# Moving weight slabs and their inputs to other byte offsets in on-chip memory

## The reference, cut to what matters

```
q, k, v = split(x @ w_qkv)            # 1024 x 3072, dilated: 1024 x 9216
gate, val = split(x @ w_in)           # 1024 x 5632
y = (gelu(conv(gate)) * val) @ w_out  # 2816 x 1024
x = layer_norm(alpha * x + y)
```

## Time and profile before

| | |
|---|---|
| median of 3 runs | 2066.23 us |
| the profiled execution | 2065.53 us, of which 2063.8 us from first to last instruction |
| TensorE matmul busy | 1916.5 us, 93% |
| GpSimd busy | 1255.1 us, 61% |
| VectorE, ScalarE busy | 1090.8 us, 999.2 us |
| HBM read | 339.65 MB, 165 GB/s over the span |

### The profile page before, as it was taken

How to read it: one execution, slowest core, us unless ns; L and a number is a source line. 1 busy time by engine, 2 the same in 40 slices (tenths; PEclk the granted TensorE clock), 3 DMA queues, 4 the chain that set the end, 5 groups by cost and what they waited for, 6 DMA issues and landing times.

```text
span 2063.8 us, 34083 instructions
## 1 busy us (share of the span) xinstructions
PE 1916.5 (93%) x13629; PEld 1696.5 (82%) x13629; DVE 1090.8 (53%) x1524; ACT 999.2 (48%) x1726; POOL 1255.1 (61%) x583
## 2 busy tenths in 40 slices
PE   7989999998999989989999899898879999998997
PEld 7879788887999866868887788876669987968996
DVE  5473346633610173146667655688665623856981
ACT  4654345543444473435553444378735545625542
POOL 8767566786888405546788334200468886426995
PEclk9999999998999999999999899999989999999999
DMA  6435367864555405358763212221235553324552
GB/s 261 142 142 184 112 259 305 319 258 153 198 190 184 143 1 194 136 216 304 311 250 143 82 64 100 82 82 62 83 132 183 183 184 143 123 82 153 189 194 106
DMA packets 49217, 342.30 MB, mean 166 GB/s; under 512 B 5264, under 2 KB 7312, under 8 KB 8144
## 3 DMA queue, kind: packets, MB, share of 16 engines
q1 hardware_dynamic: 47440, 331.02, 43.6%
q0 software_dynamic: 1664, 9.70, 1.2%
HBM read 339.65 MB, written 1.05 MB: 165 GB/s over the span
## 4 chain that ended last, share of the span: by engine, by line
PE 70%; DVE 14%; ACT 6%; POOL 6%; issue 2%; DMA 2%; DVEq 0%; SPq 0%; ACTq 0%; POOLq 0%
PE bank L1724 13%; PE bank L1726 12%; PE bank L1728 12%; PE bank L1779 10%; POOL w_lo L2232 4%; PE bank L1954 2%; PE bank L1829 2%; PE bank L1326 2%; PE bank L1328 2%; PE bank L1329 2%; PE bank L1756 2%; PE bank L1759 2%; PE bank L1758 2%; DMA ring<-slabs_dram 2%; ACT wh_area L1160 2%
## 5 line engine op out<-in xcount | busy, mean ns | idle before, releaser
L2232 POOL TENSOR_TENSOR w_lo<-ring,w_hi 128x1024 fp32r<-128x1024 f32 x360 | 876.7, 2462 | 287.7 <-ACT w_hi L2821 287.2
L1724 PE MATMUL bank<-x_hi,w_hi 128*128 128x256 f32 x2176 | 616.5, 283 | 18.1 <-POOL w_lo L2232 14.3
L1728 PE MATMUL bank<-x_lo,w_hi 128*128 128x256 f32 x2176 | 610.0, 280 | 0.0
L2821 ACT ACTIVATE w_hi<-ring 128x1024 fp32r<-128x1024 f32 x448 | 448.8, 1052 | 326.1 <-DMA ring<-slabs_dram 319.4
L1724 PEld LDWEIGHTS bank<-x_hi,w_hi 128*128 128x128 f32 x2176 | 417.5, 192 | 38.2 <-issue 36.7
L1728 PEld LDWEIGHTS bank<-x_lo,w_hi 128*128 128x128 f32 x2176 | 413.9, 190 | 0.0
L1726 PE MATMUL bank<-x_hi,w_lo 128*128 128x256 f32 x1472 | 413.4, 281 | 0.0
L1726 PEld LDWEIGHTS bank<-x_hi,w_lo 128*128 128x128 f32 x1472 | 280.9, 191 | 0.0
L2232 POOL TENSOR_TENSOR w_hi<-ring,w_hi 128x1024 fp32r<-128x1024 f32 x88 | 209.0, 2396 | 99.9 <-ACT w_hi L2821 99.9
L2745 ACT ACTIVATE arena<-bank 128x512 f32<-128x512 f32 (+1 forms) x144 | 80.0, 559 | 274.5 <-PE bank L1728 191.0
L1726 PE MATMUL bank<-x_hi,w_hi 128*128 128x256 f32 x704 | 197.1, 280 | 0.0
(11 more groups left out here) (360 smaller groups left out, 3689.0 us busy)
## 6 DMA issues: line engine op xcount, KB each, us to landing
ring<-slabs_dram SPq DMA_DIRECT2D x308, 1024.0 KB, 4.8
lnrow<-ln_dram POOLq DMA_DIRECT2D x6, 1024.0 KB, 5.0
arena<-slabs_dram SPq DMA_DIRECT2D x4, 1024.0 KB, 7.9
xt<-xT_dram SPq DMA_DIRECT2D x1, 1024.0 KB, 5.7
xt<-memT_dram SPq DMA_DIRECT2D x1, 1024.0 KB, 11.9
x<-x_dram SPq DMA_DIRECT2D x1, 1024.0 KB, 13.6
arena<-ctx_dram POOLq DMA_DIRECT2D x1, 1024.0 KB, 7.7
lnrow<-ln_dram POOLq DMA_DIRECT2D x2, 512.0 KB, 4.7
```

The costliest lines, as they stand in the source:

```text
L1724: ins = pe.matmul(dst, wh[:, k, c], src[0][:, k, :], start=(k == 0), stop=False)
L1728: ins = pe.matmul(dst, wh[:, k, c], src[1][:, k, :], start=False, stop=(k == KC - 1))
L2232: pool.tensor_tensor(dst[:, c], ring[:, s, c], w_hi[:, s, c].bitcast(F32), ALU.subtract).then_inc(S["lo_ready"], 1)
L2821: a.activation(w_hi[:, g % RING, c], ring[:, g % RING, c], ACT.Copy) \
```

## The change

Three things are reordered in the allocation. `small` shrinks from 576 to 480 floats, its columns are packed closer, and it goes to the front with 64 unused bytes behind it (`apart`); `pick` gets an area of its own where `small` was; `mod` goes behind the ring. The assertions state the outcome: `xh_area` begins 64 bytes past a multiple of 1024, and `xt2`, and with it `wh_area` and `ring`, on a multiple. By the same sums `tri`, `arena` and `x` are at 64, `dist0`, `dist` and `lnrow` at 576, `xlat`, `xt2`, `wh_area` and `ring` at 0. No instruction is added, removed or moved in any queue.

```diff
+        small = sb("small", [P, 480])
+        sb("apart", [P, 16])
         xh_at = aligned()
+        assert xh_at % 1024 == 64
         xh_area = sb("xh_area", [P, 2048])
...
         row = sb("row", [P, NROW])
-        small = sb("small", [P, 576])
-        mod = sb("mod", [P, 2, 6, 8, 2])
+        pick_area = sb("pick_area", [P, 32])
         sc_in = sb("sc_in", [P, KC, 32])
         xlat = sb("xlat", [P, KC, T])
         xt2_at = aligned()
+        assert xt2_at % 1024 == 0
...
         ring = sb("ring", [P, RING, SLAB])
+        mod = sb("mod", [P, 2, 6, 8, 2])
...
-        pick = small[:, 264:296]
-        modA = small[:, 168:184]
-        lamp = small[:, 312:440]
-        dtn = small[:, 312:568].rearrange("p (t h) -> p t h", t=4)
+        pick = pick_area[:, :]
+        modA = small[:, 152:168]
+        lamp = small[:, 216:344]
+        dtn = small[:, 216:472].rearrange("p (t h) -> p t h", t=4)
```

More of the change, by code:

```diff
@@ L263, in build @@
         half16 = small[:, 136:152]
-        pick = small[:, 264:296]
-        modA = small[:, 168:184]
-        lamp = small[:, 312:440]
-        dtn = small[:, 312:568].rearrange("p (t h) -> p t h", t=4)
[L268 to L276, removed]
+        pick = pick_area[:, :]
+        modA = small[:, 152:168]
+        lamp = small[:, 216:344]
+        dtn = small[:, 216:472].rearrange("p (t h) -> p t h", t=4)
+        epsb = small[:, 472:473]
+        sub_col = small[:, 198:199]
+        qscale = small[:, 168:176]
+        tok_i = small[:, 176:184].bitcast(I32)
+        tok_f = small[:, 184:190]
+        sq = small[:, 190:194].rearrange("p (s t) -> p s t", s=2)
+        var2 = small[:, 194:196]
+        rstd2 = small[:, 196:198]
+        dcol = small[:, 200:216]
         qT = cut(0, 8, T)
@@ L383, in build @@
         pair_sum = part("pair_sum", place(28480, 64), 64)
-        sq4 = small[:, 206:210]
+        sq4 = small[:, 190:194]
         uraw = cut(0, 8, 512)
```

## The result

The change made the kernel slower: 2079.17 us median (2074.1 to 2084.1, five runs) against 2065.68 us for the kernel before (2062.2 to 2067.2, five runs), a ratio of 1.0071 with a 95% interval of 1.0048 to 1.0094. The profile is of an execution of 2074.1 us with a span of 2072.4, the lowest of the five; the profiled execution before took 2065.5.

A forecast was written before the change was run, and what follows sets the result against it. TensorE bounds the kernel through matmul count times step. From 2065.5 us it took 15.5 us for 256-column products leaving the 117.8 ns step and nothing for the rest, giving 2050.0, range 2022 to 2082.

The forecast's parts named there:

- rival B: Every stage: the new offsets suit TensorE worse and all take the 117.8 ns step; 2087 us; chance 0.20.
- What bounds the kernel: Dense stages: TensorE never idles, so time is the number of matmuls times the step from one to the next.
- Term (1): 256-column products: 3926 of 8448 leave the 117.8 ns step for 113.3, 17.3 us, of which 15.5 us shows.
- The step behind it: `swo_tile`, 512 columns: equal offsets give 225 ns a matmul, offsets 192 apart 240; the change brings every 192 to 64.
- Term (2): 512-column products, 2016 at about 229 to 231 ns: taken as nothing; 6.5 us less if all reached 226.6.
- Term (3): Dense stages below 113.3 ns: taken as nothing; a full drop to 106.7 is 56 us, 512 columns 27 more.
- rival C: Dense stages: the new offsets also remove part of the loss in the 113.3 ns step; 2012 us; chance 0.13.
- Rival A: Dense stages: something other than offsets picks the pace, the mix stays about as now; 2066 us; chance 0.25.
- Term (5): `small`, `pick` and `mod` in new places: costed at nothing, bounds below 1 us either way.
- Term (4): Beside TensorE: GpSimd keeps its cover in h0; if DMA refused the faster slabs in f0, 4.6 us would be lost.

The follow-up runs named there:

- the sweep: Separate kernel with TensorE alone on constant data, inputs' offset varied against the weights': 113.3 to 120.0 ns at 256 columns, 226.7 to 233.3 at 512.
- the arena at distance 0: The changed kernel with the arena moved to the weights' offset modulo 256, main inputs still 64 bytes away: 2070.29 us, ratio 1.0042 to the kernel before.
- pauses: Separate kernel with TensorE alone, 256-column groups behind pauses of eight lengths at seven pairs of input and weight places: 113.3, 117.8 or 120.0 ns.
- old offsets: The changed kernel with `small` and `pick_area` behind `row`, inputs at 128 and weights at 960 as before the change: 2065.3 us, ratio 1.0001.
- another 64: The changed kernel with `small` back behind `row`, inputs at 128 and weights at 64: 2081.3 us, ratio 1.0078 to the kernel before.
- distance 0: The changed kernel's packing with `small` behind `row`, inputs and weights both at 128: 2092.24 us, ratio 1.0152 to the kernel before.
- Another 192: The changed kernel with `small` back behind `row`, inputs at 192 and weights at 0: 2062.3 us, ratio 0.9988 to the kernel before.

## Why the prediction was wrong

It said 2050 with a range of 2022 to 2082; the kernel takes 2079. The range holds it, the sign is wrong, and it came out as rival B, which had 0.20.

- **What bounds the kernel** was read rightly: the time was lost in TensorE's step alone, and the experiments reproduce the loss with no other engine at work.
- **Term (1) failed: "the slow pace at 256 columns goes".** It spread. The steady steps of 256 columns cost 17.4 us over the fast pace before and 30.5 us after; by means over three, 53% of them were fast before and 15% after. Of the three places where the prediction looked for the fall, q and k of the second dilated group fell to 113.3, and h0 and f0 did not. The cause is the distance of 64: by the sweep its usual pace with the inputs streaming is 117.8, while 192, the old one, is the best place of all with 113.3. The whole kernel with only the distance changed has the loss (1.0078), and with all but the distance changed has not (1.0001).
- **The step behind it** is the reading of the earlier trace rows: equal offsets 225 ns, 192 apart 240, so closer is better. That is two matmuls a value, from starts rounded to 10 ns, so each may be 5 ns off; over all of L1548 the steps are 228.4 ns with `w_swo` and 233.1 with `w_lo`. And it is one shape at one distance, with the weights streaming, where most products of 256 columns stream the inputs. Distance 0 is indeed the best for 512 columns (226.7; 227.3 in the kernel), but the worst for 256 columns (120.0; 119.9), where most of the time is. And no row was read for a distance of 64, so the value at 64 was a guess between two points of a curve that isn't monotonic. The 240 didn't recur as a steady step: at distance 192 it is 228.8 in the sweep.
- **Term (2), the 512-column products, was taken as 0** and measured +5.7 us: 5.9 us over twice the fast pace before, 11.6 after. The bound "if all went to 231.5, 4 us" was short, since the steady step at 64 is 233.3. With the arena at distance 0 the hidden activations' share of it came back.
- **Term (3) and rival C** (something below the fast pace): nothing did, in 16 + 4 + 6 pairs of equal offsets and 64 unequal combinations. The least is 113.3 at 256 columns; 226.7 at 512.
- **Rival A was half right.** At one distance the phase in which a stretch starts picks between two paces: same addresses, 117.9 and 113.3 (the two blocks shown under pauses). In the whole kernel "old offsets" shows the same, with h0 fast where it was slow at the same places. But the odds belong to the distance: at 192, 30 of 32 blocks with pauses fast; at 64, 15 of 16 slow. The argument "equal addresses, so addresses alone do not pick the pace" was sound, and said nothing on the odds.
- **Rival B's price, 21.5 us, was nine tenths of 19.9 + 4.** The steady steps came to +18.8 and the median to +13.5. The allowance for what borders and waits give back, a tenth, was too small here: in the profiled execution it was 10.0 of 18.8. It isn't a constant: the same subtraction gives 18.2 and -1.3 us for "another 64", 31.4 and -3.8 at distance 0, 14.8 and -9.9 for the arena at 0. What makes it -10 in two of them and -1 in another was not settled. It goes with the mean granted clock of the profiled execution: 0.972 in the two with -10, 0.969 before, 0.970 at distance 0 and 0.967 in "another 64", which over the span is some 12 us less, and up to 9 us more, at the lower level. That is one trace each, so chance of the execution and effect of the addresses aren't told apart.
- **Term (5), the moves at nothing**, held: ratio 1.0001 with both packings compared at equal offsets, and 1.0078 against 1.0071 at distance 64 with `small` behind `row` or at the front. Term (4) was not put to the test, since TensorE got slower; the windows of f0 show 309 GB/s for 314.
- **Smaller readings.** The "32 small matmuls" of an f0 slab are 16 rows in the trace; nothing was worked out from the 32. The 118.3 ns read for `half` is the 117.8 of the slow pace, from starts rounded to 10 ns.

The rule quoted in the prediction, from the Trainium skill, "SBUF — State Buffer", section "Who interferes with whom" (two independent read ports, TensorE waits on no one), would have given 2066. Taken to mean that the operands' places cost TensorE nothing, the measurement decides against it: with no other engine at work, 113.3 to 120.0 ns for the same instructions by where the two operands lie. Which of the two reads is late, no run shows.

## What to carry to other kernels

Where a trace shows the same matmuls at two steps, or a step above its columns over the clock, measure the step over the operands' places (here 26 pairs in half a millisecond) before moving anything: the curve has a period of 256 bytes, isn't monotonic, and differs with the columns and with which operand streams. A place that is good for one shape was the worst for the other, so weigh by the time in each, and give tensors of different shapes' products different places. And an effect read off one row at one distance says nothing about a third distance, nor about the sign.

## What was not expected of the hardware

**At the lower clock the distance costs nothing.** A window at a granted clock of 0.50 and two starts, 21 matmuls apart, in the kernel at distance 0 and in the kernel before, at 192:

```profile
1762.00:1767.00 5.00, 5.00 (x24) 0.50 0.60 213
...
1762.18 0.42 PE L1730 MATMUL bank<-x_hi,w_lo 128*128 128x256 f32 x1
...
1766.66 0.41 PE L1730 MATMUL bank<-x_hi,w_lo 128*128 128x256 f32 x1
```

```profile
1868.60:1873.60 5.00, 5.00 (x26) 0.50 0.57 210
...
1868.89 0.41 PE L1724 MATMUL bank<-x_hi,w_hi 128*128 128x256 f32 x1
...
1873.37 0.41 PE L1724 MATMUL bank<-x_hi,w_hi 128*128 128x256 f32 x1
```

4.48/21 is 213.3 ns in both, 256 columns at 1.2 GHz, and the kernel after, at distance 64, has 213.3 in its window from 1543 to 1548 too; at 2.4 GHz the three have 120.0, 113.3 and 117.8. What is late is late only at the upper level, which is what the prediction supposed from the earlier trace rows.

**Some steps are whole numbers of eight cycles of 2.4 GHz.** 113.3 ns is 272 cycles (256 + 16), 116.7 is 280, 120.0 is 288; at 512 columns 226.7 is 544 (512 + 32) and 233.3 is 560 (512 + 48). The others are means of steps that differ in a fixed round: 115 to 122 ns at distance 128 with 256 columns, 226 to 232 at distance 192 with 512. What sets them was not found.

**VectorE's copies changed up to sixfold, for nothing.** One step of `gated`, before, after and at the old offsets with the new packing (busy us, mean ns):

```profile
L2428 DVE CAST h_hi<-arena 128x256 f32 x40 | 41.9, 1047 | 6.2 <-DVE arena L2427 6.1
```

```profile
L2432 DVE CAST h_hi<-arena 128x256 f32 x40 | 11.8, 295 | 6.2 <-DVE arena L2431 6.1
```

```profile
L2431 DVE CAST h_hi<-arena 128x256 f32 x40 | 72.0, 1801 | 6.2 <-DVE arena L2430 6.1
```

The same cast took 1,047, 295 and 1,801 ns in the mean, the last two with the same packing, in kernels with times of 2079 and 2065. "Another 192" has 1,800, and "another 64", distance 0 and the arena at 0 have 295. So it goes with the distance and not with the packing, and the kernel before, at 192 too, lies between. The Trainium skill, "SBUF — State Buffer", section "Who interferes with whom", has VectorE and GpSimd share a port pair that a copy can find taken for the whole of the other's instruction; GpSimd works here in operations of 2.4 to 2.5 us, and a mean between 0.3 and 1.8 us would fit with how many casts fall into one. That is argued, no run isolates it. VectorE is busy half the span and nothing followed from it: the slower kernel has the faster copies.
